# Products of keys with keys and queries computed once per token tile in a chunked delta-rule stage, the stored copy used by the opposite direction

## The reference

```python
o_f = chunk_gated_delta(q, k, v, g_f, beta_f)
o_b = jnp.flip(chunk_gated_delta(jnp.flip(q, 1), jnp.flip(k, 1), jnp.flip(v, 1),
                                 jnp.flip(g_b, 1), jnp.flip(beta_b, 1)), 1)
...
gc = jnp.cumsum(g, axis=-1)
decay = jnp.exp(jnp.where(incl, gc[..., :, None] - gc[..., None, :], -jnp.inf))
kb = k * beta[..., None]
L = jnp.where(strict, jnp.einsum('bnhid,bnhjd->bnhij', kb, k) * decay, 0.0)
A = L + jnp.eye(CHUNK, dtype=L.dtype)
sol = lax.linalg.triangular_solve(A, rhs, left_side=True, lower=True, unit_diagonal=True)
intra = jnp.where(incl, jnp.einsum('bnhid,bnhjd->bnhij', q, k) * decay, 0.0)
```

## Time and profile before

| what | us |
|---|---|
| median of 3 runs | 2866.32 |
| lowest and highest of them | 2864.72, 2871.19 |
| the profiled execution, its own time | 2863.62 |
| span of the profiled execution | 2861.6 |
| PE busy | 2727.4 (95%) |
| DVE, ACT, POOL busy | 963.9, 612.1, 584.0 |

### The profile page before, as it was taken

How to read it: one execution, slowest core, us unless ns; L and a number is a source line. 1 busy time by engine, 2 the same in 40 slices (tenths; PEclk the granted TensorE clock), 3 DMA queues, 4 the chain that set the end, 5 groups by cost and what they waited for, 6 DMA issues and landing times. The chain is left out here.

```text
span 2861.6 us, 53476 instructions
## 1 busy us (share of the span) xinstructions
PE 2727.4 (95%) x18871; PEld 1372.9 (48%) x18871; DVE 963.9 (34%) x2089; ACT 612.1 (21%) x1838; POOL 584.0 (20%) x969
## 2 busy tenths in 40 slices
PE   8999999999999999999898999999999999999997
PEld 4544455556676676676563455332333233333332
DVE  1135444431364464464654235311111111111100
ACT  4100355521322322413310111311111111111100
POOL 1445111102222322323510000211111111211111
PEclk9999999999999999999998999999999999999999
DMA  7664100021220221210516448799999999999996
GB/s 248 216 220 149 56 29 30 22 91 31 73 58 29 70 60 37 61 31 23 191 68 260 162 143 341 317 411 406 405 397 407 383 406 383 409 380 395 394 412 230
DMA packets 170387, 603.44 MB, mean 211 GB/s; under 512 B 16527, under 2 KB 81895, under 8 KB 116455
## 3 DMA queue, kind: packets, MB, share of 16 engines
q1 hardware_dynamic: 163175, 587.08, 53.3%
q0 software_dynamic: 6912, 12.59, 2.5%
HBM read 553.65 MB, written 45.98 MB: 210 GB/s over the span
## 5 line engine op out<-in xcount | busy, mean ns | idle before, releaser
L2749 PE MATMUL psum<-wbuf 128*32 128x512 f32 x2976 | 347.4, 608 | 35.8 <-issue 34.0
L2749 PE MATMUL psum<-x,wbuf 128*32 128x512 f32 x3024 | 340.0, 592 | 0.0
L1458 PE MATMUL psum<-xT,wbuf 128*128 128x512 f32 x720 | 336.8, 606 | 0.3 <-PEq L831 0.3
L718 POOL COPY wbuf<-xT 128x16 f32 x533 | 114.5, 215 | 782.5 <-issue 430.8
L2749 PEld LDWEIGHTS psum<-wbuf 128*32 128x32 f32 x2976 | 113.0, 112 | 259.0 <-issue 259.0
L2749 PEld LDWEIGHTS psum<-x,wbuf 128*32 128x32 f32 x3024 | 114.7, 110 | 211.9 <-issue 211.9
L718 DVE COPY wbuf<-xT 128x16 f32 x500 | 95.0, 191 | 339.9 <-issue 339.0
L1458 PEld LDWEIGHTS psum<-xT,wbuf 128*128 128x128 f32 x720 | 132.1, 192 | 128.1 <-issue 122.4
L2766 PE MATMUL psum<-x,hT 128*32 128x512 f32 x1584 | 177.9, 592 | 0.0
L718 ACT COPY wbuf<-xT 128x16 f32 x503 | 111.3, 221 | 275.7 <-issue 272.5
L2766 PE MATMUL psum<-wbuf,hT 128*32 128x512 f32 x1488 | 167.5, 592 | 2.1 <-DVE ye L2836 2.1
(11 more groups left out here) (328 smaller groups left out, 3386.8 us busy)
## 6 DMA issues: line engine op xcount, KB each, us to landing
x<-in_w_down SPq DMA_DIRECT2D x66, 1024.0 KB, 11.2
wbuf<-in_w_gate SPq DMA_DIRECT2D x65, 1024.0 KB, 9.3
wbuf<-in_w_up SPq DMA_DIRECT2D x65, 1024.0 KB, 12.0
x<-in_w_gate SPq DMA_DIRECT2D x63, 1024.0 KB, 9.7
x<-in_w_up SPq DMA_DIRECT2D x63, 1024.0 KB, 11.9
wbuf<-in_w_down SPq DMA_DIRECT2D x62, 1024.0 KB, 10.8
wbuf<-in_w_in SPq DMA_DIRECT2D x16, 2048.0 KB, 9.2
wbuf<-weight_sums SPq DMA_DIRECT2D x16, 2048.0 KB, 9.2
```

What stands on the lines that cost most here:

```text
L718: last = copy(k.xeT[:, half, :, t:t + 1], k.mixT[:, :, cols][:, :, bass.ds(r, 1)])
L1458: last = nc.tensor.matmul(ps[:, b, 0:SS_], wg[:, m % 2, d, h * P:(h + 1) * P], k.xT[:, d, SP_:T], start=(d == 0), stop=(d == KD - 1))
L2749: last = nc.tensor.matmul(ps[32 * j:32 * j + 32, g, :].rearrange("p (x c r) -> p x c r", x=2, r=32), xeT[:, half, q, 32 * g:32 * g + 32], ...
```

## The change

For each pair of heads `gram` is called twice instead of three times. It computes the products of groups 0 and 1, and then those of group 3 alone. ScalarE copies each of these three results from PSUM into SBUF (`save_gram`, after `lower` of the group has read them), into parts of `obuf` and `inv` that are free at that time. `lower` of groups 2, 4 and 5 reads the stored copy of its twin (0, 3 and 1), with the two directions exchanged, in place of PSUM, and waits for the copy. TensorE waits for the copies in two places before it overwrites the banks: in `v_transposes` for groups 0 and 1, and in part 1 of the scan of group 1 for group 3. What `gram(i, 2)` waited for (the output of group 1 stored, its state updated, L1501 and L1502) is waited for there no longer, nor are the first inverses at L1505.

```diff
+        gram_tile = lambda v: v.rearrange("p h (q c) -> p h q c", q=2)
+        by_tile = obuf.rearrange("p d t h c -> p d t (h c)")
+        saved = {0: [gram_tile(by_tile[:, 1, 0:2]), gram_tile(by_tile[:, 1, 4:6])],
+                 1: [gram_tile(by_tile[:, 1, 2:4]), inv[:, 8 * P:12 * P].rearrange("p (h q c) -> p h q c", h=2, q=2)],
+                 3: [gram_tile(by_tile[:, 0, 3:5]), gram_tile(by_tile[:, 0, 1:6:4])]}
+        twin = {2: 0, 4: 3, 5: 1}
+        grams = list(saved)
...
                 def v_transposes(i):
                     pe.wait_ge(s_silu, i * NC + 6)
                     pe.wait_ge(s_lt, i * NG + 2)
+                    pe.wait_ge(s_gs, i * 3 + 2)
...
                 def gram(i, r):
                     if r == 0:
                         pe.wait_ge(s_nrm, i * 4 + 4)
-                    elif r == 2:
-                        pe.wait_ge(s_oc, i * NG + 2)
-                        pe.wait_ge(s_st, i * n_sn + sn_at(1))
                     else:
                         pe.wait_ge(s_kvc, i * 6 + 6)
-                        for x in range(2):
-                            pe.wait_ge(s_tt[x], i * 18 + 1)
-                    for x in range(2):
-                        tiles = group_tiles(2 * r + x)
+                    for g in ((0, 1), (3,))[r]:
+                        tiles = group_tiles(g)
...
# scan(i, g, part) on TensorE, part 1
                         pe.wait_ge(s_tf, i * NG + g + 1)
+                        if g == 1:
+                            pe.wait_ge(s_gs, i * 3 + 3)
...
                         round_(i, r)
                         if r < 2:
-                            gram(i, r + 1)
+                            if r == 0:
+                                gram(i, 1)
...
+                def save_gram(i, g):
+                    act.wait_ge(s_lt, i * NG + g + 1)
+                    for d in range(2):
+                        m = ps[:, 4 + 2 * (g % 2) + d, :].rearrange("p (h q c) -> p h q c", h=2, q=2)
+                        last = nc.scalar.copy(saved[g][d], m)
+                    last.then_inc(s_gs, 1)
...
                     for b in range(3):
                         store_kv(i, b)
+                    save_gram(i, 0)
+                    save_gram(i, 1)
                     if more:
                         copy_tile(i + 1, 1)
...
+                        if r == 0:
+                            save_gram(i, 3)
                         if r < 2 and more:
                             copy_tile(i + 1, 2 + r)
...
# lower(i, g) on VectorE
-                    dve.wait_ge(s_gram, i * NG + g + 1)
+                    if g in twin:
+                        dve.wait_ge(s_gs, i * 3 + grams.index(twin[g]) + 1)
+                    else:
+                        dve.wait_ge(s_gram, i * 3 + grams.index(g) + 1)
...
-                        m = ps[:, 4 + 2 * x + d, :].rearrange("p (h q c) -> p h q c", h=2, q=2)
+                        m = (saved[twin[g]][1 - d] if g in twin
+                             else ps[:, 4 + 2 * x + d, :].rearrange("p (h q c) -> p h q c", h=2, q=2))
```

More of the change, by code:

```diff
@@ L1332, in deltanet @@
         s_gram = sem("gram")
+        s_gs = sem("gram_saved")
         s_dtin = sem("decay_masked")
@@ L1511, in gram @@
                             for h in range(2):
-                                last = nc.tensor.matmul(ps[:, 4 + 2 * x + d, 2 * h * P:2 * (h + 1) * P], kq[:, h, 0, cols],
+                                last = nc.tensor.matmul(ps[:, 4 + 2 * (g % 2) + d, 2 * h * P:2 * (h + 1) * P], kq[:, h, 0, cols],
                                                         kq[:, h, :, cols], start=True, stop=True)
```

## The result

The changed kernel takes 2825.49 us (median of 4 runs, 2824.65 to 2830.46), and the kernel before 2865.52 us on the same chip (2864.19 to 2871.19): 0.9858 of the time, 95% interval 0.9842 to 0.9874. That is 40 us less. The forecast was 2855, 10 us less, with a range of 2844 to 2861. The direction was right, and the size was outside the range.

What follows compares the result with a forecast made beforehand. TensorE was taken to bound the DeltaNet block (busy 208.28 of 213.80 us per pair). Terms 1.5 + 10.35 + 0 - 1.7 gave 10.2 us off, 2853.4 or 2856.1 by base, taken as 2855, range 2844 to 2861.

Steps and rivals of the forecast that it cites:

- 1.5 + 10.35 + 0 - 1.7 = 10.2 us off: Whole kernel: savings of the DeltaNet block's pairs added up and subtracted from the profiled 2863.62 us, giving 2853.4.
- Between rounds 0 and 1: First three pairs: VectorE's 2.28 us head start loses 1.8 to SBUF contention, leaving 0.5 us (0.2 to 0.8) each.
- Between rounds 1 and 2: First three pairs: VectorE is ready 1.6 us before TensorE despite contention, so the full 3.45 us each, 10.35 in all.
- The last pair: Last pair of heads: no gain from the removed matmuls and some loss, -1.7 us (-3.2 to 0.2).
- The loss that I described: Last pair, round 2: TensorE does one product, idles some 3 us, perhaps then runs at 1.2 GHz, 1.4 us at even chance.
- 10.9 and 0.62 us of waits of TensorE: DeltaNet block: TensorE waits 10.9 us before output transposes and 0.62 at round 1's first level; other engines' charges are slack.
- The copies: ScalarE: 24 copies of 0.59 us, 14.2 us on an engine idle for 70%, costed at nothing.
- A: The forecast itself, with contention in `lower`: 2855 us, 2850 to 2859, chance 0.70.
- B: VectorE's reads of stored products stay at 0.36 us, no contention: 20.6 us off, 2843.0 or 2845.7, chance 0.20.
- C: Contention makes VectorE late in round 2 too, using up the 3.45 us: no change, 2863 to 2866, chance 0.07.
- D: VectorE's operations take 1.92 us, late by 6.8 in round 2, low clock behind: slower, 2884 us, chance 0.03.
- The errata section named in the prediction: VectorE: fixed 58 cycles from SBUF against 120 from PSUM, about 65 ns shorter per operation, sum 1 us better; not adopted.

Runs made afterwards that it cites:

- e1: Kernel before with 60 idle semaphore increments on TensorE, moving the experts' loop to 231 instructions ahead of a block's end: 2842.91 us, 0.9909 of before.
- e2: Changed kernel with 196 idle semaphore increments on TensorE, putting the experts' loop back at the instruction number it had before: 2855.05 us, 0.9948 of before.
- e7: Kernel before with 28 idle semaphore increments on TensorE, putting the loop's head 7 instructions ahead of a block's end: 2873.64 us, 1.0028 of before.
- e10: e5 with 104 idle semaphore increments on TensorE, putting the loop's head 127 instructions ahead of a block's end: 2822.92 us, 0.9843 of before.
- e3: Kernel before with TensorE's loop over pairs of experts written out, so nothing jumps back: 2841.06 us, 0.9904 of before.
- e4: Changed kernel with TensorE's loop over pairs of experts written out: 2825.82 us, 0.9856 of before.
- e5: Changed kernel with GpSimd's `decay_kq` in rounds 1 and 2 waiting for the first inverse of the round's second group: 2820.04 us, 0.9841 of before.
- e9: e5 with TensorE's loop over pairs of experts written out as in e4: 2816.06 us, 0.9823 of before.
- e6: Changed kernel with group 2's products computed again and read from PSUM, groups 4 and 5 still reading copies: 2831.56 us, 0.9881 of before.
- e8: Kernel before with ScalarE's copies and TensorE's two waits added, copies unread, plus 52 idle semaphore increments: 2839.78 us, 0.9911 of before.

## Why the prediction was right in direction and wrong in size

**The step that failed** is the sum: "1.5 + 10.35 + 0 - 1.7 = 10.2 us off. From the profiled execution's own 2863.62 that is 2853.4". It subtracts what the DeltaNet block saves from the whole span, so it takes everything behind the block as merely shifted. The removed matmuls are also removed instructions. They move the head of the experts' loop from 35 to 231 instructions ahead of a block's end, which takes away the second stop in each of six turns. e1 and e2 show it in both directions, e7 and e10 at two more places, and e3 and e4 that without the jump there is no stop. It is worth 16.6 us of the profiled 37.7. The stops themselves shrink by 34.0 - 23.7 = 10.3 us; the rest is what stands behind them: before, the 48 records took 8.7 us with the second stop in them, 7.05 after, and 5.36 in the second turn of e1, which is their time at the full clock. The 34.0 us of idle time before `up` were in the profile before, at the top of the list of costly groups, and I hadn't read them, since they weren't in the stage that the edit names.

The Trainium skill has the rule, in "Runtime: NRT & Kernel Launch", section "Instruction fetch mechanics": code is fetched in blocks of 256 instructions one after the other, and a jump to a place outside the blocks held has to wait for its block. The first stop in each turn, 3.3 to 4.1 us, agrees with it: the loop is 2332 instructions long, more than the 2048 that the section gives for TensorE. No run here has a shorter loop. That the next block can be late as well is what e7 shows beyond it.

**Between rounds 0 and 1**, predicted 0.5 us for each of three pairs: measured 0.95, 1.16 and 0.79 (0.2 to 0.8 was the range), from `gram` to TensorE's first update of round 1 (13.08 to 12.13 in the first pair, 792.91 to 805.99 and 789.37 to 801.50). The mechanism was right: VectorE's head start goes partly to contention, and TensorE's wait grows, from 0.62 to 1.40 us, where "nearly 2" was expected. Only the size was off: 0.80 us for an operation was the guess, 0.65 is what four of them took.

**Between rounds 1 and 2**, predicted 3.45 us for each of three pairs: right. In the first pair the way from the first update of round 1 to the first product of round 2 was 40.51 us (805.99 to 846.50) and is 37.06 (801.50 to 838.56), 3.45 less. From one round 0's `gram` to the next pair's the first two pairs are 4.27 and 4.33 us shorter, which is 3.45 and the 0.95 and 1.16 above within 0.3. TensorE runs into no wait there:

```profile
838.56 1.15 PE L1526 MATMUL psum<-inv,mix_g 64*64 64x64 f32 x32
839.63 2.05 PE L1552 MATMUL psum<-state,wbuf 128*128 128x128 f32 x16
```

VectorE is ready at 835.98, 2.6 us earlier, although all eight operations read SBUF; their spacing is 0.39 to 0.87.

**Between the third and the last pair** 2.3 us more came than I had foreseen (the third pair is 6.53 us shorter, of it 3.45 and 0.79 explained). The wait before the last pair's first `gram` fell from 4.81 to 3.44, and the output transposes from 2.82 to 2.51 us. What `gram` waits for is `normalise` on VectorE, an operation on 128x768 elements with its operands in SBUF. Its last two, before and then after:

```profile
1361.38 4.54 DVE L1905 SCALAR_TENSOR_TENSOR wbuf<-wbuf,mix_g 128x768 f32<-128x768 f32 x2 [5.39 <-ACT mix_g L1739]
```

```profile
1344.07 1.02 DVE L1926 SCALAR_TENSOR_TENSOR wbuf<-wbuf,mix_g 128x768 f32<-128x768 f32 x1 [4.46 <-ACT mix_g L1749]
1345.89 1.35 DVE L1926 SCALAR_TENSOR_TENSOR wbuf<-wbuf,mix_g 128x768 f32<-128x768 f32 x1 [0.79 <-ACT mix_g L1749]
```

From the start of the first to the end of the second it is 4.54 us in before, e1, e3, e5 and e9, and 3.15 to 3.54 in after, e2, e4, e6, e7, e8 and e10. e7 and e8 don't contain the change, and e5 and e9 do, so the change as such doesn't decide it. Without the change the third pair takes 195.7 us with the longer form and 193.4 (e7) and 192.4 (e8) with the shorter. So the 2.3 us are luck. GpSimd works on its convolution of 128x772 elements at the same time; that what matters is how the two lists happen to meet is likely, and no run shows it.

**The last pair**, predicted -1.7: measured 0.0 (146.68 to 146.70 us). The loss that I described is there, but something else makes up for it. From the second `gram` of the pair on, the rest lost 1.76 us (105.54 to 107.30). The front, from the first `gram` to the second, gained 1.74 (41.14 to 39.40): the first `gram` there takes 3.72 us in place of 5.88, and the granted clock of that stretch is 0.91 in place of 0.86. The wait ahead of it was shorter, as said above, and the front goes with it in every kernel: 41.1 to 41.2 us in the five with the longer form of `normalise`, 38.9 to 40.8 in the others. So the front's gain is luck too, and what the change did here is the loss. TensorE does one product of round 2 and then waits 3.15 us, where "some 3" was said, and the granted clock behind it is at the lower level, 1.2 GHz, part of the time:

```profile
1427.24 0.68 PE L1526 MATMUL psum<-inv,mix_g 64*64 64x64 f32 x16
1431.07 1.12 PE L1526 MATMUL psum<-inv,mix_g 64*64 64x64 f32 x16 [3.15 <-DVE inv L1962]
```

```profile
1430.50:1434.00 3.50, 2.93 (x25) 2.81 (x26) 1.81 (x5) 0.00 (x0) 0.00 (x0) 0.56 0.00 0
```

Before round 1, where a gain of 0 was forecast, there is the same wait in small, 1.84 us. The prediction named 10.9 and 0.62 us of waits of TensorE and took the rest for slack. The same view of the kernel before also has 7.6 us for `inv`, 6.0 of them before the first product of this pair, and 4.8 before its first `gram`, and in that place the front and the third pair gained:

```profile
PE psum L1519 <- DVE inv L1937: 7.6, 3, 6.0
PE psum L1512 <- DVE wbuf L1905: 4.8, 1, 4.8
```

**The block in all.** Of its 15 us, some 4 (2.3 and 1.7) are luck in this sense, and some 11 are the change, where 10.2 were forecast, with bounds of 7.7 and 12.9. Against e7 and e8, which have the shorter form of `normalise` and not the change, the kernel after gains 12.9 and 8.8 us in the block.

**The copies**, costed at nothing: right, by e8. In the first pair the copies of group 3 started at 797.47, and `copy_tile` behind them at 798.43. That is 1 us later than before in a block that began 3.6 us sooner, so the queue was held for some 4.6 us (5.3 were forecast), and no wait of TensorE for it appears.

```profile
797.47 1.07 ACT L1761 COPY wbuf<-psum 128x512 f32<-128x512 f32 x2 [10.88 <-DVE mix_g L1948]
798.43 0.60 ACT L1714 COPY pre<-psum 128x512 f32<-128x512 f32 x1
```

**The rivals.** A was right in the mechanism of the DeltaNet block. B (no contention, 2843) is refuted by the rows of L1944 and by e5, which takes part of the contention away and gains 7.3 us, although its 2843 is nearer to the time measured; C and D didn't come. None of them spoke of the experts.

**The Trainium skill's rule** on shared SBUF access ("SBUF — State Buffer", section "SBUF: two separate sides") bore out: in e5 the operations with two SBUF operands that no longer run beside `decay_kq` fell to 0.41 us, and those beside `beta_inverse` stayed at 0.62. The errata section named in the prediction has them 65 ns shorter than from PSUM (an estimate from its cycles); undisturbed L1945 takes 410 ns, and from PSUM 405 to 415, so the rows still don't show it.

**The other two stretches.** The 3.6 us ahead of the DeltaNet block are the same code in both kernels. From 300 to 400 us of the span the granted clock is 0.95 before and 0.98 after. But the clock alone doesn't account for it: e3, with 0.95, has 615.4 us ahead of the block, and e1, with 0.98, 615.6. With the change the stretch is 613.3 to 613.6 us in after, e4, e5 and e9 and 616.6 to 617.1 in e2, e6 and e10; without it, 615.3 to 616.9. So the change alone doesn't decide it, and what does stays open, with one profiled execution of each kernel. The 2.5 us in the routing also vary between 390.5 (e7, without the change) and 394.3 (e2, with it).

## What to carry to other kernels

An edit that adds or removes instructions shifts all code behind it on that engine. If a hardware loop follows, look at its waits on "issue" in the profile before the edit, and price them for the case that they move: here 17 to 33 us of the experts' stage hung on 28 to 196 instructions, more than on the arithmetic that the change saved. When a version seems better or worse, rerun it with a few dozen idle instructions ahead of the loop, or with the loop written out, before crediting the edit. And when a product is moved from PSUM into a stored copy, look for the engine that works in SBUF at the same time; a single wait that puts it behind the critical operations gave 7.3 us of the DeltaNet block here (5.5 between the medians).

## What the runs showed of the hardware that was not expected

- Each jump back of 2332 instructions on TensorE is followed by a stop of 3.3 to 4.1 us. If the target is 35 instructions ahead of the end of a block of 256, a second stop of 1.3 to 3.3 us follows, and with 7 instructions one of 4.0 to 4.8. With 127 and more (e10, e6, e1, e8) there was none. The end of the block is where e7 and the kernel before place it.
- The stage follows: 922.8 us (231 instructions), 922.3 (235), 922.4 (167, e6), 923.7 (127), 939.4 and 947.5 (35), and 954.8 us (7), with the same loop.
- With no stop at all (e3, e4, e9) the stage is 920.1 to 922.2 us, with the transfers of weights at some 410 GB/s and TensorE waiting for them, 17.7 us in e3.
- After waits of 3.44 us (after), 3.69 (e8) and 4.81 (before) of TensorE ahead of the same eight matmuls, these took 3.72, 5.41 and 5.88 us.
- VectorE's elementwise products of 128x256 elements (L1944, L1945) take 0.41 us alone with both operands in SBUF, 0.62 beside GpSimd's 128x128 operations and up to 0.95 beside its 128x256 ones; with one operand in PSUM they take 0.38 to 0.43 in all cases.
